# First projections and a gate moved from the start of each attention stage into the tail of the stage before

## What is computed

```python
z = h @ lp['w_in']        # split into the inputs and the gates of four groups
q_mla = (rmsnorm(m_cq, ...) @ lp['mla_wq_b'])      # mla: latent q and kv, 4 heads
gq = rmsnorm(g_q...); gk = rmsnorm(g_k...)         # gqa: 4 query heads, 2 key heads
a = (p[:, :, 0] - lam * p[:, :, 1])                # diff: two softmaxes per head
o = concatenate([o_mla * silu(m_gate), o_gqa * silu(g_gate),
                 o_diff * silu(d_gate), o_hy * silu(hy_gate)])
x = x + gate * rmsnorm(o @ lp['w_out'], ...)
```

## Time and profile before

| | us |
|---|---|
| median of three runs | 2669.18 |
| lowest, highest | 2665.99, 2670.72 |
| the profiled execution, its time | 2677.52 |
| its span, first to last instruction | 2675.7 |
| PE busy in it | 2401.0 (90%) |
| VectorE, ScalarE busy | 1318.8 (49%), 909.3 (34%) |
| mean granted clock of TensorE | 0.956 |

### The profile page before, as it was taken

How to read it: one execution, slowest core, us unless ns; L and a number is a source line. 1 busy time by engine, 2 the same in 40 slices (tenths; PEclk the granted TensorE clock), 3 DMA queues, 4 the chain that set the end, 5 groups by cost and what they waited for, 6 DMA issues and landing times. The chain is left out here.

```text
span 2675.7 us, 36353 instructions
## 1 busy us (share of the span) xinstructions
PE 2401.0 (90%) x14472; PEld 1609.8 (60%) x14472; DVE 1318.8 (49%) x2642; ACT 909.3 (34%) x1826; POOL 172.6 (6%) x183
## 2 busy tenths in 40 slices
PE   3999999898999887979949999998989999889798
PEld 1755775675466676764417557656844667767543
DVE  3352663564556376581133526645644653855711
ACT  1142112442245264471012421134521542745600
POOL 0220001000100000001202200000010000000012
PEclk8999999899999998999959999999999999989999
DMA  6440000100100000102145301001001000001021
GB/s 221 151 160 26 30 22 17 49 1 14 34 32 1 12 1 6 65 2 87 63 155 185 126 26 52 16 1 49 1 14 34 32 1 12 1 6 65 3 100 55
DMA packets 74225, 129.11 MB, mean 48 GB/s; under 512 B 24994, under 2 KB 38178, under 8 KB 72420
## 3 DMA queue, kind: packets, MB, share of 16 engines
q1 hardware_dynamic: 73944, 122.04, 13.2%
q10 hardware_dynamic: 112, 4.72, 0.5%
HBM read 109.54 MB, written 21.92 MB: 49 GB/s over the span
## 5 line engine op out<-in xcount | busy, mean ns | idle before, releaser
L601 PE MATMUL psum<-arena 128*32 128x128 f32 (+8 forms) x9904 | 1733.7, 405 | 117.4 <-DMA arena<-in_hy_decay 48.3
L601 PEld LDWEIGHTS psum<-arena 128*128 128x128 f32 (+3 forms) x9904 | 1048.5, 155 | 742.3 <-issue 520.7
L605 PE MATMUL psum<-ident,arena 128*128 128x128 f32 (+1 forms) x2248 | 356.3, 284 | 92.7 <-ACT arena L1381 38.4
L1561 DVE TENSOR_TENSOR arena<-arena 128x64 f32<-128x64 f32 (+10 forms) x670 | 301.8, 497 | 183.5 <-ACT arena L1508 59.3
L605 PEld LDWEIGHTS psum<-ident,arena 128*128 128x128 f32 (+1 forms) x2248 | 256.3, 142 | 196.1 <-issue 106.2
L601 PE MATMUL psum<-k_parts,q_parts 96*128 96x384 f32 (+2 forms) x1000 | 286.2, 375 | 15.8 <-ACT k_parts L1495 4.6
L1561 DVE TENSOR_TENSOR arena<-psum,arena 128x512 f32<-128x512 f32 (+2 forms) x116 | 67.1, 580 | 279.2 <-PE psum L601 278.8
L1853 DVE TENSOR_REDUCE st<-psum 128x1 f32<-128x1152 f32 (+1 forms) x144 | 177.9, 1237 | 50.5 <-PE psum L601 50.0
L601 PEld LDWEIGHTS psum<-k_parts,q_parts 96*128 96x128 f32 (+1 forms) x1000 | 171.4, 195 | 33.3 <-issue 18.1
L1913 DVE TENSOR_REDUCE st<-psum 128x1 f32<-128x1152 f32 (+1 forms) x144 | 173.2, 1233 | 36.4 <-PE psum L601 36.1
L1319 ACT ACTIVATE arena<-psum,st 128x1152 f32<-128x1152 f32 (+1 forms) x144 | 162.3, 1127 | 76.1 <-DVE st L1853 72.7
(11 more groups left out here) (132 smaller groups left out, 1328.7 us busy)
## 6 DMA issues: line engine op xcount, KB each, us to landing
arena<-in_ada_w SPq DMA_DIRECT2D x12, 2048.0 KB, 8.9
arena<-in_w_in SPq DMA_DIRECT2D x10, 2048.0 KB, 9.0
arena<-out_xs SPq DMA_DIRECT2D x36, 512.0 KB, 4.2
out_xs<-arena SPq DMA_DIRECT2D x18, 512.0 KB, 2.6
arena<-in_w_out SPq DMA_DIRECT2D x4, 2048.0 KB, 8.5
out_xs<-in_x ACTq DMA_DIRECT2D x1, 4608.0 KB, 19.0
spectrum_kept<-arena SPq DMA_DIRECT2D x2, 2304.0 KB, 8.1
arena<-spectrum_kept SPq DMA_DIRECT2D x2, 2304.0 KB, 8.5
```

The source lines that it names most:

```text
L601: return nc.tensor.matmul(out, lhsT, rhs, start=start, stop=stop)
L605: return nc.tensor.transpose(out, src, ident[0:n, 0:n])
L1561: return nc.vector.tensor_tensor(out, a, b, op)
```

## The change

`AHEAD = {"mla": 2, "gqa": 2, "diff0": 3, "diff1": 3}` token tiles of each attention stage are projected in the tail of the stage before. For mla they stand on PE ahead of the last transposes of hyena (`out_tile`), in banks 6 and 7, and those transposes go round six banks (`K.front()`). For gqa they stand at steps `len(units)` and `len(units) + 2` of mla's attention, for diff0 at three steps from `len(units)` of gqa's, for diff1 at three steps from `len(units) + 2` of diff0's. The three gate pieces of diff1 are made at three steps from `len(units)` of diff0's attention, in banks 3 to 5; ScalarE's tanh (`tanh_ahead`, into the memory of the queries) and VectorE's multiply (`gate_ahead`) move into the same tail. In the preparations the projection in step `i` is that of tile `i + AHEAD - 1`, so it stands `AHEAD - 1` tiles ahead of the turn beside it. The last steps then have no projection; in gqa two gate pieces stand there, in diff0 `prompt_values` and one gate piece, in diff1 nothing. `K.restart` sets where the banks go on. Copies, norms and turns of a tile stay in their stage.

```diff
+AHEAD = {"mla": 2, "gqa": 2, "diff0": 3, "diff1": 3}
...
+                weights("mla")
+                for t in range(AHEAD["mla"]):
+                    project("mla", "proj", t, "mla", 0, 416, [6 + t])
                 for t in range(TT):
-                    out_tile("hy", t, zv[:, t, 2, :], K.next())
+                    out_tile("hy", t, zv[:, t, 2, :], K.front())
...
+                        if g == len(units):
+                            pe.wait_ge(*S.at("exps", (grp, g - 2)))
+                            pe.wait_ge(*S.at("exps", (grp, g - 1)))
+                        if grp == "mla" and g in (len(units), len(units) + 2):
+                            weights("gqa")
+                            project("gqa", "proj", (g - len(units)) // 2, "gqa", 0, 512, [(g - len(units)) // 2])
+                        if grp == "gqa" and len(units) <= g < len(units) + 3:
+                            weights("diff")
+                            diff_project("diff0", g - len(units), [g - len(units)])
...
+                        if grp == "diff0" and len(units) <= g < len(units) + 3:
+                            gate("diff", "diff_vg", GW, 1, g - len(units), [3 + g - len(units)])
+                        if grp == "diff0" and len(units) + 2 <= g < len(units) + 5:
+                            diff_project("diff1", g - len(units) - 2, [g - len(units) - 2])
...
-                    if i < TT:
-                        project("mla", "proj", i, "mla", 0, 416)
+                    if AHEAD["mla"] <= i < TT:
+                        project("mla", "proj", i, "mla", 0, 416, K.next())
...
+                        t = i + AHEAD[grp] - 1
+                        if AHEAD[grp] <= t < TT and grp == "gqa":
+                            project(grp, "proj", t, grp, 0, 512, K.next())
+                        elif AHEAD[grp] <= t < TT:
+                            diff_project(grp, t, K.next())
+                        if grp == "gqa" and i >= NT:
+                            gate("gqa", "gqa_gate", 0, 0, i - NT, K.next())
+                        if grp == "diff0" and i == NT:
+                            prompt_values()
+                        if grp == "diff0" and i == TT:
+                            gate("diff", "diff_vg", GW, 0, 0, K.next())
                         if i >= 1:
                             parts_turned(grp, i - 1)
...
+                        if grp == "diff0" and g == len(units) + 2:
+                            for i in range(3):
+                                tanh_ahead(i)
...
+                        if grp == "diff0" and g == len(units) + 3:
+                            for i in range(3):
+                                gate_ahead(i)
```

More of the change, by code:

```diff
@@ L774, in _ @@
                 for t in range(2):
[L775 removed]
+                    project("hy", "gate", t, "hy1", 256, GW, K.next())
                 to_tokens(5)
@@ L1109, in _ @@
                     for i in range(TT + 1):
-                        if i < TT and grp == "gqa":
-                            project(grp, "proj", i, grp, 0, 512)
-                        elif i < TT:
-                            ps = claim(("proj", grp, i), K.next())
-                            for k in range(KD):
-                                w = W[:, SLOT["diff", 0], k, :].rearrange("p (a b n) -> p a b n", a=2, b=2)
-                                last = mm(ps[:, 0:256], hT[:, k, i * P:(i + 1) * P], w[:, :, int(grp[4]), :],
-                                          k == 0, k == KD - 1)
-                            last.then_inc(*K.done(("proj", grp, i)))
+                        t = i + AHEAD[grp] - 1
[9 more added lines that the diff above has]
+                            gate("diff", "diff_vg", GW, 0, 0, K.next())
                         if i >= 1:
@@ L2090, in _ @@
                             gate_finish("gqa", f, i, six, OT + 2 * TOK)
-                    else:
-                        f = int(grp[4])
+                    elif grp == "diff0":
                         for i in range(3):
-                            gate_finish("diff", f, i, [(f, i) for i in range(3)], OT + 4 * TOK)
+                            gate_finish("diff", 0, i, [(0, i) for i in range(3)], OT + 4 * TOK)
                     if grp == "diff0":
```

46 lines of the change are left out of this document (32 added, 14 removed).

## The result

The changed kernel takes 2683.37 us (median of 5 runs, 2682.09 to 2691.17) against 2669.89 of the kernel before (five runs; the 2669.18 above was the median of three): ratio 1.0061, 95% interval 1.0047 to 1.0075. It is slower, by more than the 0.2% that can be told from no change. The forecast was 2680.4, in a range of 2667 to 2692, with 0.68 on slower.

The account below looks back on a forecast made before the run. TensorE bounds the kernel (busy 2401.0 of 2675.7 us), so only its idle and low-clock time counts. Terms 5.0 + 0.4 + 1.7 - 1.5 give 5.6 per layer, 11.2 for two, on the 2669.18 median: 2680.4 us, range 2667 to 2692.

Parts of the forecast that it names:

- 5.08 + 1.7 + 0.78: Per layer: gqa's last-turn wait of 5.08 us, low clock behind it 1.7, and diff0's last-turn wait 0.78 all go.
- The bookkeeping by kind: Per layer, PE idles about 10 us more and gets some 4.5 us back from the clock.
- Mla, +5.0: Start of mla: stage starts 11.5 us later, second transpose comes 6.7 earlier within it; net +5.0 us per layer, up to +6.5.
- Gqa, +0.4: Start of gqa: stage starts 12.6 us later, 12.1 saved inside; net +0.4 us per layer, from -1.5 to +3.
- about 1.0 is filled: Tail of mla: of 1.80 us of PE holes, about 1.0 is filled by the gqa projections moved there.
- Diff0, +1.7: Start of diff0: stage starts 9.35 us later, 7.6 saved inside, first turn stays at +13.05; net +1.7 us per layer.
- Diff1, -1.5: Start of diff1: start moves by 20.8 us, preparation gives back 22.3; net -1.5 us per layer, from -3 to +1.5.
- The -22.3: Diff1's preparation: time saved before attention with gates and three projections gone, 22.3 us per layer.
- +37: Diff1: attention begins about 37 us after the stage start instead of 58.83, last turns taking some 1.2 us each.
- The clock: Low-clock terms kept, one low stretch per long hole; without them the sum is +20 us, 2689 us.
- the fast case: Rival: filled tails and shorter holes keep the clock up, new holes cost no low stretch; 2660 us, chance 0.12.
- the slow case: Rival: behind 8 to 11 us holes 5.1 us lost instead of 1.75 in three stages; 2700 us, chance 0.12.

Follow-up runs that it names:

- The four kernels in a chain: Kernel before plus gate pieces between last turns, 2649.24 us; plus diff1's gate in diff0's tail, 2648.67; plus gqa, diff0, diff1 projections ahead, 2672.18; plus mla's, 2683.37.
- the experiment: Changed kernel with only its mla part undone (both mla projections back in mla's own stage): 2672.18 us, ratio 1.0006 to the kernel before.
- third experiment: Kernel before with gate pieces between the last turns and diff1's gate in diff0's tail, no projection ahead: 2648.67 us, ratio 0.9921.
- the copy experiment: Changed kernel with ScalarE copying the next tile's projection before moving the turned tile in gqa, diff0 and diff1: 2678.6 us, ratio 1.0026.
- the kernel with all covers: Changed kernel with mla's projections back, gate pieces first in gqa and diff0, early ScalarE copies, gqa's wait where loads are used: 2635.53 us, ratio 0.9871.

## Why the prediction was right, point by point

**The four kernels in a chain** give the price of each part (medians, both layers): gate pieces between turns -20.5, diff1's gate in diff0's tail -0.6, projections of gqa, diff0 and diff1 ahead +23.5, those of mla ahead +11.2. The sum is +13.6 against 13.5 measured; each price is uncertain by some 4 us. In the forecast's own terms, per layer: the pieces were worth 5.08 + 1.7 + 0.78 = 7.6, and 10.2 was measured; mla ahead 5.0, and 5.6; the rest, 5.6 + 7.6 - 5.0 = 8.2, and 11.5. So the total was right partly by luck: a gain and a loss were both put too low. The table by place says the same, with misses from -4.6 to +3.7 us that cancel.

**The bookkeeping by kind** held: 10 us more idle per layer (9.75 by the page), 4.5 back from the clock (4.45 by the page, 3.0 if the medians are taken). By place, in layer 0, idle rose 4.6 in front of mla's attention (forecast 5.3), 4.8 in gqa (3.4), 1.4 in diff0 (2.7) and 0.1 in diff1 (-1.5).

**Mla, +5.0.** The first transpose was forecast at +8.4 of the stage's start and came at +8.1 (421.15 - 413.03); the 9.05 idle take in the 0.96 at the end of hyena. The second was forecast at +13.3 and came at +14.5. The 1.2 us between are the low clock behind the longer hole: the expansion takes 4.61 us there and 9.03 - 5.75 = 3.3 in the earlier trace rows. The size is 5.6 by the experiment, 6.5 and 5.4 by the traces; the forecast allowed for up to 6.5.

**Gqa, +0.4; measured -1.9 and -4.2.** The first turn came at +19.07 (forecast +18.34; the load landed at +11.1, before the change at +10.4, and in the traces it lands anywhere from +9.7 to +12.4), the waits of 5.08 and the low stretch behind went. Mis-sized: "about 1.0 is filled" of mla's tail. PE idled 4.88 in mla's attention before and 5.02 after: nothing was filled. And the clock gave more than 1.7: it was 0.96 in mla's attention before and 0.99 after, in layer 1 0.97 and 1.00. That this comes from the change can't be said, for in the kernels without projections ahead it was 0.97 and 0.96 in layer 0 and 1.00 in layer 1.

**Diff0, +1.7; measured +1.8 and +4.2.** First turn at +11.97 behind 8.28 idle, for +13.05 behind 9.4. The gate piece filled the 0.78. In layer 1 gqa's attention, tail included, grew by 12.0 us where 9.35 was forecast; its granted clock was 0.96 there and 0.99 before, which the change isn't shown to cause.

**Diff1, -1.5; measured +2.2 and +1.7: the step that failed.** The start moved by 21.4 us (forecast 20.8) and the preparation gave back 19.2 (22.3). The -22.3 doesn't follow from the forecast's own +37, which gives 37 - 58.83 = -21.8 and a net of -1.0, so 0.5 us of the miss is a slip in the sum. The tail filled as forecast (idle 19.74 to 15.01 in diff0's attention and tail), though 2.0 us stayed idle where under 1.5 was given. The projections lay over ScalarE's last two table loads, one over that ahead of the logarithm and two over that ahead of the exponential; without them (third experiment) that chain costs 2.4 us and a low clock behind. The first turn came at +6.3 (forecast +6.75). But "then the last turns by themselves at some 1.2 each ... attention at about +37" assumed that VectorE would have its tiles ready. ScalarE's order kept it from that: 2.77 us of wait, with a low clock behind it, and 39.6 for 37; the copy experiment gave back 3.2 and 3.4 us.

**The clock.** The forecast kept terms for it against the Trainium skill ("TensorE: Matmul & The Clock Gate", Part 1), which advises against fitting the moment at which the throttle lets go; without them it would have been 2689. The page of after has PE busy 8.9 us less with the same instructions, by the medians some 6.0 is left of that (forecast 9), and 2680.4 is nearer to 2683.4 than 2689 is. But single places moved by 2 to 4 us between executions with nothing changed there, which agrees in kind with what the Trainium skill says of that moment, that it varies from run to run. The terms had the right sign in the sum; place by place they don't hold.

**Rivals.** The clock did not go up enough for the fast case (a mean of 0.952 for after against 0.956; that mean counts idle time too, which is why it can fall while PE is busy less: it is 0.74 from 654.43 to 673.50, though the 7.11 us of work in there ran at full speed and the other 11.96 are idle). Behind the holes of 8 to 12 us it was low for a turn and a projection, 2.0 us lost in gqa of layer 0 (1.97 + 8.06 for 1.04 + 7.03) and 1.6 to 2.7 at the other three, not 5.1 as the slow case had it.

## What to carry to other kernels

Work moved out of a stage's start is only won if what it covered there is gone too: look for the load that ends the first wait, and ask what PE does until it lands. Fill such a wait with work that needs none of the loads and that another engine can finish at once; and move a wait on loads behind every step that doesn't read them. A cover over another engine's chain must be queued behind the instruction that starts the chain, and a function of another table set inside that chain costs a load for itself and one for each function behind it. Don't count on the clock in this: whether it fell behind a short wait differed from layer to layer.

## What the runs showed of the hardware

**The low clock behind a wait.** What a hole costs in clock is the time of the first turn and of the projection behind it, less what they take at the full clock (1.04, and 7.03 in gqa or 3.62 in diff). Behind the first-turn holes of 4.2 to 12.3 us in the twelve traces it was 1.6 to 3.1 us, and not in order of length: 1.96 behind 11.96, 3.10 behind 12.10, 1.82 behind 12.33, 1.87 behind 5.23, 2.73 behind 7.70. Behind holes of 2.6 to 3.7 us there were two outcomes and nothing between them: 1.5 us or more in 22 cases, under 0.1 in 12. The same place in the two layers of the kernel with all covers shows both:

```profile
891.50 1.60 PE L610 MATMUL psum<-ident,split_buf 128*96 128x128 f32 x8 [2.71 <-DVE split_buf L1616]
892.89 4.81 PE L606 MATMUL psum<-arena 128*128 128x256 f32 x16
...
2200.97 1.08 PE L610 MATMUL psum<-ident,split_buf 128*96 128x128 f32 x8 [2.72 <-DVE split_buf L1616]
2201.89 3.62 PE L606 MATMUL psum<-arena 128*128 128x256 f32 x16
```

The granted clock is 1.00 ahead of both holes, then 0.73 over the first pair and 1.00 over the second. So shortening a long hole gives back its idle time for certain, and the clock only where it happens not to fall. That this also spreads the times of one kernel is likely and not shown, since each kernel has one trace.

**Table loads.** ScalarE's table load took 1.28 us wherever it was shown, and three tanh between two rounds of logarithm and exponential caused three of them: one ahead of the tanh, and one each ahead of the last logarithm and the last exponential, where everything waits. Without the tanh there the same two functions ran with none.
